# Turning three quarters of the residual through a DRAM scratch instead of on TensorE

## The reference

```python
x = x + mixed @ w_out[l]                                   # mixed: 256 x 2048
mem_n = rms_norm(mem, norm_mem_src[l])
x = x + memory_cross_attention(rms_norm(x, norm_mem_x[l]), mem_n, w_mem_q[l], w_mem_kv[l], w_mem_o[l])
#   in it: q = h @ w_q,  w_q: 2048 x 512
x = x + hierarchical_moe(rms_norm(x, norm_ffn[l]), ...)    # w_gate, w_up, w_down of 32 experts
```

## Time and profile before

| What | Value |
|---|---|
| Median of the runs | 1350.66 us |
| Profiled execution: time, span | 1350.58 us, 1348.8 us |
| TensorE busy in the span | 992.5 us (74%) |
| VectorE, ScalarE busy | 576.0 us (43%), 303.9 us (23%) |
| DMA | 486.40 MB, mean 361 GB/s |

### The profile page before, as it was taken

How to read it: one execution, slowest core, us unless ns; L and a number is a source line. 1 busy time by engine, 2 the same in 40 slices (tenths; PEclk the granted TensorE clock), 3 DMA queues, 4 the chain that set the end, 5 groups by cost and what they waited for, 6 DMA issues and landing times.

```text
span 1348.8 us, 20643 instructions
## 1 busy us (share of the span) xinstructions
PE 992.5 (74%) x8516; PEld 595.7 (44%) x8516; DVE 576.0 (43%) x1132; ACT 303.9 (23%) x537; POOL 40.9 (3%) x92
## 2 busy tenths in 40 slices
PE   8999999999999975666555666655566655566656
PEld 7888898888888522222222222212222222222222
DVE  5555567776656643233322233332223332223324
ACT  5554457774544100000000000000000000000002
POOL 1300000130000000000000000000000000000001
PEclk9999999999999997778777778787787787777878
DMA  7777764447869999999999999999999999999997
GB/s 245 262 243 250 214 176 125 152 150 276 290 235 354 359 432 429 434 431 432 430 432 434 430 430 430 434 431 430 430 435 431 431 431 431 434 431 430 430 427 307
DMA packets 78021, 486.40 MB, mean 361 GB/s; under 512 B 9944, under 2 KB 25438, under 8 KB 64799
## 3 DMA queue, kind: packets, MB, share of 16 engines
q1 hardware_dynamic: 77484, 483.46, 89.0%
q10 hardware_dynamic: 306, 2.11, 0.4%
q0 software_dynamic: 192, 0.31, 0.2%
HBM read 481.14 MB, written 4.72 MB: 360 GB/s over the span
## 4 chain that ended last, share of the span: by engine, by line
PE 50%; DMA 46%; SPq 1%; DVE 1%; issue 1%; ACT 0%; DVEq 0%; ACTq 0%
DMA gu<-in_w_up 42%; PE ps L1053 10%; PE ps L606 8%; PE ps L608 8%; PE ps L607 8%; PE ps L1108 5%; DMA down<-in_w_down 4%; PE ps L1032 2%; PE ps L1065 1%; PE ps L586 1%; PE ps L851 1%; PE ps L852 1%; PE ps L853 1%; PE ps L778 1%; SPq L471 0%
## 5 line engine op out<-in xcount | busy, mean ns | idle before, releaser
L1053 PE MATMUL ps<-gu,xe 128*32 128x256 f32 x3968 | 284.9, 450 | 305.8 <-DMA gu<-in_w_up 305.3
L2144 DVE TENSOR_TENSOR x_sum<-ps,x_sum 128x512 f32<-128x512 f32 x240 | 149.1, 684 | 508.3 <-PE ps L1065 508.3
L1053 PEld LDWEIGHTS ps<-gu,xe 128*32 128x32 f32 x3968 | 139.7, 129 | 468.9 <-DMA gu<-in_w_up 328.5
L1619 DVE TENSOR_TENSOR w_lo<-w_raw,w_hi 128x1024 fp32r<-128x1024 f32 (+1 forms) x137 | 164.6, 1207 | 117.7 <-ACT w_hi L1226 114.2
L606 PE MATMUL ps<-w_hi,a_hi 128*128 128x512 f32 (+1 forms) x468 | 183.3, 392 | 0.0
L607 PE MATMUL ps<-w_lo,a_hi 128*128 128x512 f32 (+1 forms) x468 | 179.8, 384 | 0.0
L608 PE MATMUL ps<-w_hi,a_lo 128*128 128x512 f32 (+1 forms) x460 | 176.8, 384 | 0.0
L1226 ACT ACTIVATE w_hi<-w_raw 128x1024 fp32r<-128x1024 f32 (+1 forms) x137 | 141.9, 1040 | 128.7 <-PE ps L608 98.2
L1538 ACT ACTIVATE sg<-ps 128x128 f32<-128x128 f32 x31 | 8.6, 278 | 654.3 <-PE ps L1053 654.3
L1108 PE MATMUL ps<-down,act_t 128*32 128x512 f32 x976 | 112.4, 601 | 6.1 <-DMA down<-in_w_down 6.1
L607 PEld LDWEIGHTS ps<-w_lo,a_hi 128*128 128x128 f32 x468 | 88.0, 188 | 16.4
(11 more groups left out here) (335 smaller groups left out, 831.6 us busy)
## 6 DMA issues: line engine op xcount, KB each, us to landing
down<-in_w_down SPq DMA_DIRECT2D x29, 4096.0 KB, 22.7
gu<-in_w_gate SPq DMA_DIRECT2D x28, 4096.0 KB, 31.7
gu<-in_w_up SPq DMA_DIRECT2D x28, 4096.0 KB, 40.9
w_raw<-in_w_in SPq DMA_DIRECT2D x56, 512.0 KB, 5.1
w_raw<-in_w_out SPq DMA_DIRECT2D x32, 512.0 KB, 4.4
gu<-in_w_up SPq DMA_DIRECT2D x18, 512.0 KB, 6.1
w_raw<-in_w_mem_kv SPq DMA_DIRECT2D x16, 512.0 KB, 3.5
down<-in_w_down SPq DMA_DIRECT2D x13, 512.0 KB, 15.2
```

What stands on the lines that cost most here:

```text
L1053: mm = pe.matmul(ps[5][j * SLOTS:(j + 1) * SLOTS, 0:2 * P].rearrange("s (m f) -> s m f", m=2), xe[:, k, :], gu[side][:, :, k, j * P:(j + 1 ...
L1619: ve.tensor_tensor(w_lo[:, u % RING, :, 0:n], w_raw[:, u % RING, :, 0:n], w_hi[:, u % RING, :, 0:n], ALU.subtract).then_inc(S("w_split"), 1)
L2144: ins = ve.tensor_tensor(x_sum[:, t, cols], ps[g][:, :], (x_res if first else x_sum)[:, t, cols], ALU.add)
```

## The change

Quarters 0 to 2 (`X_QUADS = 3`) are no longer turned on TensorE. ScalarE stores the finished quarter of `x_res` to three new places of the scratch (`spill_x`) and reads it back in four pieces into the first half of `nat` (`read_x`), both from its own DMA queue. VectorE turns it into the second half (`memx_turn`), with every fourth feature next to each other, so that partition p holds features 4p to 4p + 3 of the quarter. ScalarE and VectorE make high parts and rests from there, with a gain `g_x` loaded in the same order, and the rows of `w_mem_q` for these units are loaded four to a partition. TensorE's wait for twelve rests before chunk 25 stays.

```diff
-        SPLIT_BANK.append(6 + _b % 2 if _name == "mem" else 4 + _b % 4)
+        SPLIT_BANK.append(None if _name == "memx" and _i < UK * X_QUADS else
+                          6 + _b % 2 if _name == "mem" else 4 + _b % 4)
...
+        x_quads = nat[:, 0].rearrange("p t (j f) -> p (t j) f", f=P)
+        x_t = nat[:, 1].rearrange("p t (k j s) -> p (t k) j s", k=UK, s=QUAD)
...
+            if c == MEM_Q and i < UK * X_QUADS:
+                q, b = divmod(i, UK)
+                return [w_mem_q[0, q * UN:(q + 1) * UN, :].rearrange(
+                    "(p k) n -> p k n", k=NJ)[:, b * UK:(b + 1) * UK, :]]
...
+                sp.dma_start(g_x[:, :, :], norm_mem_x[0, 0:X_QUADS * UN].rearrange("(q p k) -> p q k", p=P, k=NJ)
+                             ).then_inc(S("ffn_gain_loaded"), 16)
...
                 project(W_OUT + 2 * q)
-                pe.wait_ge(*chunk_out(W_OUT + 2 * q - 1))
-                if q == 1:
-                    pe.wait_ge(S("sums_made"), 1)
-                split_turn("memx", x_res, 4 * (q - 1), 4 * q)
                 project(W_OUT + 2 * q + 1, a0=HEADS)
...
             def memx_heads(q):
+                if q == X_QUADS:
+                    split_head("memx", 32, hi=a2_hi, k_from=4 * q, k_to=4 * q + 4)
+                else:
+                    sc.wait_ge(S("quads_turned"), X_MOVED + q + 1)
+                    for k in range(NJ):
+                        sc.activation(a2_hi[:, 4 * q + k, :], x_t[:, k].rearrange("p j s -> p (j s)"), ACT.Copy,
+                                      scale=g_x[:, q, k:k + 1]).then_inc(S("split_hi"), 1)
                 x_squares(q, junk1)
+            def spill_x(q):
+                sc.wait_ge(*chunk_out(W_OUT + 2 * q + 1))
+                sc.dma_start(spill[X_MOVED + q].rearrange("(t p) f -> p t f", p=P),
+                             x_res[:, :, q * UN:(q + 1) * UN]).then_inc(S("spilled"), 16)
+            def read_x(q):
+                sc.wait_ge(S("spilled"), 16 * (X_MOVED + q + 1))
+                sc.wait_ge(S("quads_turned"), X_MOVED + q)
+                for i in range(NJ):
+                    sc.dma_start(x_quads[i * QUAD:(i + 1) * QUAD, :, :],
+                                 spill[X_MOVED + q, :, i * P:(i + 1) * P].rearrange("(j s) f -> s j f", s=QUAD)
+                                 ).then_inc(S("quads_loaded"), 16)
             for c in range(W_OUT, MEM_Q):
+                q, g = divmod(c - W_OUT, 2)
+                if q >= 1:
+                    rounded(START[c] + 1 + RING)
+                    if g == 0:
+                        spill_x(q - 1)
+                        rounded(START[c] + 3 + RING)
+                        read_x(q - 1)
+                    else:
+                        memx_heads(q - 1)
                 rounded(DONE[c] + RING)
-                if c > W_OUT and (c - W_OUT) % 2 == 0:
-                    memx_heads((c - W_OUT) // 2 - 1)
...
+            def memx_turn(q):
+                ve.wait_ge(S("quads_loaded"), 16 * NJ * (X_MOVED + q + 1))
+                if q >= 1:
+                    ve.wait_ge(S("split_lo"), SPLIT0["memx"] + 4 * q)
+                ve.transpose(x_t, x_quads.rearrange("p j (r k) -> p k j r", k=NJ)).then_inc(
+                    S("quads_turned"), 1)
...
             for c in range(W_OUT, MEM_Q):
+                q, g = divmod(c - W_OUT, 2)
+                if q >= 1 and g:
+                    split_w(START[c] + 1 + RING)
+                    memx_turn(q - 1)
+                    split_w(START[c] + 2 + RING)
+                    memx_rests(q - 1)
                 split_w(DONE[c] + RING - (1 if c == W_OUT else 0))
                 add_heads(c)
-                if c > W_OUT and (c - W_OUT) % 2 == 0:
-                    memx_rests((c - W_OUT) // 2 - 1)
```

More of the change, by code:

```diff
@@ L98 @@
 MOVE_AT = [DONE[_c] + RING + 3 for _c in QUADS]
+X_QUADS = 3
+X_MOVED = len(QUADS)
 NAT = {SB_Q: 0, SB_Q + 1: 1, SB_K: 0, SB_K + 1: 1, KV_LAT: 0, Q_PE: 1, MEM_K: 0, MEM_Q: 1}
@@ L174, in layer @@
         g_ffn = place("g_ffn", [P, KD])
+        g_x = place("g_x", [P, X_QUADS, NJ])
         sums = place("sums", [P, 16])
@@ L272, in layer @@
         ps = [ctx.enter_context(nc.psum_tensor(f"ps{i}", [P, 512], F32)) for i in range(8)]
-        spill = nc.dram_tensor("spill", (len(QUADS), SEQ, UN), F32, kind="Internal").ap()
+        spill = nc.dram_tensor("spill", (X_MOVED + X_QUADS, SEQ, UN), F32, kind="Internal").ap()
+        x_quads = nat[:, 0].rearrange("p t (j f) -> p (t j) f", f=P)
+        x_t = nat[:, 1].rearrange("p t (k j s) -> p (t k) j s", k=UK, s=QUAD)
         def quads_of(n):
@@ L439, in _ @@
                 if u == last_units:
+                    sp.wait_ge(S("quads_turned"), X_MOVED + X_QUADS)
                     load_piece(1, 1, 8, 10)
@@ L836, in _ @@
             pe.wait_ge(*chunk_out(MEM_Q - 1))
+            pe.wait_ge(S("sums_made"), 1)
             split_turn("memx", x_res, KD - 4, KD)
@@ L868, in mem_scores @@
                 pe.wait_ge(S("turn_copied"), bank0[MEM_Q] + t + 1)
-                pe.wait_ge(S("quads_turned"), len(QUADS))
+                pe.wait_ge(S("quads_turned"), X_MOVED)
                 for p in range(2):
@@ L1450, in memx_heads @@
             def memx_heads(q):
-                split_head("memx", 32, hi=a2_hi, k_from=4 * q, k_to=4 * q + 4)
-                x_squares(q, junk1)
-            for c in range(W_OUT, MEM_Q):
+                if q == X_QUADS:
[5 more added lines that the diff above has]
+                                      scale=g_x[:, q, k:k + 1]).then_inc(S("split_hi"), 1)
+                x_squares(q, junk1)
+            def spill_x(q):
[9 more added lines that the diff above has]
+                                 ).then_inc(S("quads_loaded"), 16)
+            sc.wait_ge(S("ffn_gain_loaded"), 32)
+            for c in range(W_OUT, MEM_Q):
+                q, g = divmod(c - W_OUT, 2)
[7 more added lines that the diff above has]
+                        memx_heads(q - 1)
                 rounded(DONE[c] + RING)
-                if c > W_OUT and (c - W_OUT) % 2 == 0:
-                    memx_heads((c - W_OUT) // 2 - 1)
             rounded(START[MEM_Q] + 3 + RING)
@@ L1462, in _ @@
             sc.wait_ge(S("rstd"), 6)
-            sc.wait_ge(S("quads_turned"), len(QUADS))
+            sc.wait_ge(S("quads_turned"), X_MOVED)
             sc.wait_ge(S("queries_made"), 1)
@@ L1866, in x_sums @@
                                  chunk_ss[:, :, :], AX, ALU.add).then_inc(S("sums_made"), 1)
-            def memx_rests(q):
-                split_rest("memx", 32, hi=a2_hi, lo=a2_lo, k_from=4 * q, k_to=4 * q + 4)
+            def memx_turn(q):
[4 more added lines that the diff above has]
+                    S("quads_turned"), 1)
+            def memx_rests(q):
+                if q == X_QUADS:
+                    split_rest("memx", 32, hi=a2_hi, lo=a2_lo, k_from=4 * q, k_to=4 * q + 4)
+                    return
+                for k in range(NJ):
+                    ve.wait_ge(S("split_hi"), SPLIT0["memx"] + 4 * q + k + 1)
+                    ve.scalar_tensor_tensor(
+                        out=a2_lo[:, 4 * q + k, :], in0=x_t[:, k].rearrange("p j s -> p (j s)"),
+                        scalar=g_x[:, q, k:k + 1], in1=a2_hi[:, 4 * q + k, :], op0=ALU.mult,
+                        op1=ALU.subtract).then_inc(S("split_lo"), 1)
             ve.wait_ge(S("rstd"), 5)
             for c in range(W_OUT, MEM_Q):
+                q, g = divmod(c - W_OUT, 2)
[4 more added lines that the diff above has]
+                    memx_rests(q - 1)
                 split_w(DONE[c] + RING - (1 if c == W_OUT else 0))
@@ L1876, in _ @@
                     turn_quads(QUADS.index(MEM_K))
-                if c > W_OUT and (c - W_OUT) % 2 == 0:
-                    memx_rests((c - W_OUT) // 2 - 1)
+            ve.sem_inc(S("split_turned"), UK * X_QUADS)
             split_w(START[MEM_Q] + 3 + RING)
@@ L2068, in turn_slots @@
                 return ve.tensor_tensor(xe[:, k0:k1, :], xe_raw[:, k0:k1, :], bc(gb, kn, SLOTS), ALU.mult)
-            ve.wait_ge(S("ffn_gain_loaded"), 16)
+            ve.wait_ge(S("ffn_gain_loaded"), 32)
             for n, (bank, k0, k1) in enumerate(FIRST_PARTS[0:2]):
```

## The result

The changed kernel took 1379.46 us (median of 6 runs, 1374.55 to 1381.64) against 1351.25 us of the kernel before beside it (6 runs, 1350.42 to 1352.66): ratio 1.0203, interval 1.0193 to 1.0214. The forecast was 1353.9 us, at most 1359.5. Its side was right; its size, +3.3 us, is 12% of the +28.2 measured. The profiled execution has a span of 1376.3 us, 27.5 more than before.

A forecast was written before the change was run, and what follows sets the result against it. TensorE bounds the kernel up to about 440 us, the experts' weights afterwards. The profiled 1350.58 us plus 2 x 4.5 - 5.7 = +3.3 us, the 2.6 us saving included, gave 1353.9 us; range 1350.4 to 1359.5.

The forecast's parts named there:

- The saving: Three groups of eight transpositions leave TensorE's queue between 320 and 370 us: 3 x 0.87 = 2.6 us, all on the path.
- What it adds beside other work: VectorE transpositions of 1.24 us each, changed copies, 3.1 MB more traffic: engines have room, DMA share about 0.95.
- The order of the trip: Store, read back, VectorE's transposition, ScalarE's high parts, VectorE's rests, in program order: 19.0 + s us per third against TensorE's 21.8.
- the formula 2s - 5.7: How many us later than before chunk 25's first unit begins on TensorE, s being a store's time: +3.3 at 4.5.
- The size of s: Time for a 512 KB scratch store from ScalarE's queue to land: 4.5 us taken, between ends of 2.3 and 6.4.
- The reads: "6, hidden": Each trip's four reads back from scratch land within 6 us with competing traffic, against 6.7 us allowed.
- The first third, called covered: First trip, after chunk 18's add: store and reads have 12.3 us until VectorE's transposition can start at 326.9 us.
- Late reads: Rival: stores of 6.2 us and reads of 7.7, beyond the 6.7 allowed, give 1359.3 us; chance 0.16.
- unit 17: Counted from chunk 19's first as 0; split after the second loop's first rests, late for TensorE if reads overrun further.
- The argument against late reads: The SP queue's loads are not urgent, since each has a ring of four units.

The follow-up runs named there:

- unused transfers: Kernel before, TensorE's groups kept, the three stores and twelve reads added on ScalarE's queue, nobody using what is read: 1351.53 us, ratio 0.9997.
- the short transfers: Changed kernel with every store and read of the three trips cut to 64 bytes a row: 1359.43 us, ratio 1.0053.
- the filler: Changed kernel with matmuls on the identity before TensorE's wait ahead of chunk 25: with 100, 1375.03 us, ratio 1.0176; with 200, 1386.63 us, ratio 1.0260.

## Why the prediction was wrong, step by step

- **The saving** held: three groups gone; where nothing waits, a group is worth what its row said (1.65 us for two).
- **"What it adds beside other work"** held for traffic (0.9997 with unused transfers) and failed for the transposition: 1.99 us, not the 1.24 taken, though the stated bound, twice 1.24, covers it. It stands on the path, 2.2 us in three.
- **The order of the trip** held. With the measured stores and the slower transpositions, the formula 2s - 5.7 gives the wait of the short transfers within 0.1 us, and the chain has the forecast's steps in their order with nothing else between them.
- **The size of s** failed: 7.45 us instead of 4.5, beyond the upper end of 6.4. It was read from DMAs between 73 and 258 us, and its fixed part, "about 2 us", from reads in front of which SP had issued nothing for 6 us (the store at 73.16, the reads at 79.58 us). In this stretch 8 KB take 4.0 to 5.8 us.
- **The reads: "6, hidden"** is the step that failed most: 14.0, 9.5 and 11.2 us from the first issue, 15.6 us of the 22.8. Here too the 2.3 to 3.3 us of the earlier trace rows carried it. The first third, called covered, has 8.3 of the 15.6: store and reads took 20.35 us against 12.3 of cover. Late reads were a rival, but with 7.7 us and a price of 1.0 per trip, and without the first third, where its own 6.2 + 7.7 passes the cover by 1.6; and a late read moves the roundings and splits behind it too: unit 17, which that rival named, and unit 9, which it did not.
- **Missing was the restart of TensorE**, 2.3 us for units begun at half clock behind the last wait, of which the filler gave 2.1 back. At units 9 and 17 the clock fell too, but there the trip was the path.
- The argument against late reads, that SP's loads are not urgent, was beside the point: SP kept issuing them, and the reads shared the engines with them. With fewer the reads came sooner (e.g. 8.4 instead of 14.0 us).

The Trainium skill, page "DMA: Bandwidth & Descriptors", section on the anatomy of one DMA, has about 2.0 us plus the bytes at 436 GB/s for a DMA issued from GpSimd; by that the estimate is 3.2 us for 512 KB and 2.0 for 8 KB. The runs disagree: 6.3 to 7.4 us for the stores from GpSimd's queue, and from ScalarE's, which the section is not about, 6.3 to 7.5 and 4.0 to 5.8. The same page's section on latency has the access to HBM at 0.2 us on average and 2 us at high load, which goes in the runs' direction without reaching their size.

What stays open is how the engines share among queues. One read of 512 KB landed sooner than four of 128 KB, eight landed no later than four, and identical reads scatter between 8 and 14 us from kernel to kernel. That the bytes queued beside them do it, three runs show together: with nothing issued ahead of them on SP's queue the same reads take 2.3 to 3.3 us each, from GpSimd's queue beside SP's loads they are late again, and with fewer loads the stores land sooner. By what rule isn't shown.

## What to carry to other kernels

Take a DMA's landing from rows of the stretch where it will stand, with the traffic of that stretch: a fixed cost of 2 us, read where nothing else was queued, was 4.0 to 5.8 here. A trip through memory takes work off the busiest engine only if its use stands later than the slowest landing seen (here 14 us) with some margin; with 17 us it won 0.24%, with 6.7 it lost 2%. And where a chain of stages repeats, write the loop down and ask what each microsecond of error in its terms does, since every trip pays it again.

## Not expected of the hardware

- A transposition of 128x1024 on VectorE takes 1.98 to 2.04 us when it reads every fourth 4-byte element, and 1.25 when it reads consecutive ones. The Trainium skill, page "SBUF — State Buffer", section "Specifications (TRN2)", says that this memory has lines of 16 bytes and gives full bandwidth from two hits on a line; a step of 16 bytes has one, and the trace agrees.
- In a stretch where the DMA share is near 1, the size of a transfer tells little of its landing: 8 KB 4.0 to 5.8 us, 128 KB 5.5 to 12.5, 512 KB 5.2 to 7.9 in one read (with pieces of 4 KB instead of 512 bytes).
- Behind waits of 5 to 12 us TensorE's granted clock read 0.50 to 0.57, and its 512-column matmuls came 0.43 us apart (the chain's last row) instead of 0.23 (2.726 us for the 12 of a unit).
